# Gathering a token's lower-numbered expert row during the last expert of a two-layer MoE backbone

## The reference, cut to what matters

```
def moe_route(flat, router_w, router_b):
    s = jax.nn.sigmoid((flat @ router_w).astype(jnp.float32))
    ...
    _, idx = lax.top_k(jnp.where(in_group, biased, -jnp.inf), TOP_K)
    w = jnp.take_along_axis(s, idx, axis=-1)
    w = w / jnp.sum(w, axis=-1, keepdims=True)
...
    for e in range(N_EXPERTS):
        hid = jax.nn.silu(flat @ w_gate[e]) * (flat @ w_up[e])
        out = out + combine[:, e:e + 1] * (hid @ w_down[e]).astype(jnp.float32)
...
    x = x + g1 * mx
    x = x + g2 * moe_ffn(...)
```

## Time and profile before

| | us |
|---|---|
| Median of three executions | 1182.84 |
| Lowest and highest | 1179.83, 1184.31 |
| Profiled execution, its own time | 1181.55 |
| Span in its trace | 1179.6 |
| PE busy | 1021.6 (87%) |
| DVE busy | 927.7 (79%) |
| ACT busy | 607.1 (51%) |
| POOL busy | 164.7 (14%) |

### The profile page before, as it was taken

One profiled execution on the slowest core, in us unless ns is written; L12 is line 12 of the kernel. 1 busy time (PEld: TensorE's weight loads), 2 busy tenths in 40 slices (PEclk: granted clock), 3 DMA queues, 4 the chain that ended last, 5 costly groups with the idle time before them and its releaser, 6 DMA issues. The chain is left out here.

```text
span 1179.6 us, 13718 instructions
## 1 busy us (share of the span) xinstructions
PE 1021.6 (87%) x4742; PEld 778.9 (66%) x4742; DVE 927.7 (79%) x1041; ACT 607.1 (51%) x614; POOL 164.7 (14%) x172
## 2 busy tenths in 40 slices
PE   6889999998898982999999999838299999999970
PEld 1466767766565441788888888637278888888860
DVE  4578888877894336699999999655769999999955
ACT  1534222213664113677777777333367777777831
POOL 0100200000100002612212210041341000000005
PEclk9899999998999995899999999959599999999985
DMA  9615878676014004899999999567299999999936
GB/s 372 261 62 208 285 284 302 224 279 232 4 69 134 36 25 155 278 410 414 413 414 414 413 414 414 210 248 278 93 263 404 414 414 414 414 414 414 413 132 234
DMA packets 145692, 332.43 MB, mean 282 GB/s; under 512 B 14064, under 2 KB 16056, under 8 KB 145520
## 3 DMA queue, kind: packets, MB, share of 16 engines
q1 hardware_dynamic: 125768, 277.99, 62.0%
q10 hardware_dynamic: 12392, 28.68, 6.5%
q0 software_dynamic: 7488, 25.19, 5.7%
HBM read 308.72 MB, written 23.15 MB: 281 GB/s over the span
## 5 line engine op out<-in xcount | busy, mean ns | idle before, releaser
L1879 DVE TENSOR_TENSOR w_lo<-ring,w_hi 128x2048 fp32r<-128x2048 f32 x192 | 430.5, 2284 | 24.5 <-ACT w_hi L1725 21.1
L1725 ACT CAST w_hi<-ring 128x2048 fp32r<-128x2048 f32 x192 | 365.3, 1914 | 132.6 <-PE bank L1970 38.7
L1970 PE MATMUL bank<-w_hi,xT_hi 128*128 128x512 f32 x512 | 205.3, 401 | 8.2 <-DVE xT_lo L1886 8.2
L1970 PE MATMUL bank<-w_hi,xT_lo 128*128 128x512 f32 x512 | 201.4, 393 | 0.0
L1970 PE MATMUL bank<-w_lo,xT_hi 128*128 128x512 f32 x512 | 200.9, 392 | 0.0
L1399 PE MATMUL bank<-ring_last_parts,arena_parts 128*128 128x512 f32 (+1 forms) x320 | 116.8, 396 | 5.0 <-DVE ring_parts L1016 2.7
L1970 PEld LDWEIGHTS bank<-w_hi,xT_hi 128*128 128x128 f32 x512 | 97.2, 190 | 30.1 <-DVE xT_lo L1886 9.8
L1970 PEld LDWEIGHTS bank<-w_hi,xT_lo 128*128 128x128 f32 x512 | 96.9, 189 | 21.2
L1970 PEld LDWEIGHTS bank<-w_lo,xT_hi 128*128 128x128 f32 x512 | 97.4, 190 | 19.2
L1074 DVE SCALAR_TENSOR_TENSOR gate_b<-ring,silu_c,gate_b 128x512 f32<-128x512 f32 x140 | 105.9, 756 | 4.5
L1985 PE MATMUL bank<-w_hi,hT_hi 128*128 128x512 f32 x256 | 101.5, 396 | 7.5 <-DVE w_lo L1879 7.5
(11 more groups left out here) (252 smaller groups left out, 1379.3 us busy)
## 6 DMA issues: line engine op xcount, KB each, us to landing
ring<-in_moe_w_gate SPq DMA_DIRECT2D x64, 1024.0 KB, 11.0
ring<-in_moe_w_up SPq DMA_DIRECT2D x64, 1024.0 KB, 13.0
ring<-in_moe_w_down SPq DMA_DIRECT2D x64, 1024.0 KB, 10.7
ring<-in_ada_w SPq DMA_DIRECT2D x21, 2048.0 KB, 8.9
y_scratch<-shared ACTq DMA_DIRECT2D x32, 512.0 KB, 6.0
ring<-in_w_in ACTq DMA_DIRECT2D x21, 512.0 KB, 3.8
shared<-in_ada_w SPq DMA_DIRECT2D x2, 2048.0 KB, 16.0
x_res<-in_x SPq DMA_DIRECT2D x8, 512.0 KB, 12.3
```

The lines of the kernel that those rows point to most:

```text
L1725: nc.scalar.copy(w_hi[:, buf(u, p), :], half(raw(e, p))).then_inc(s_hi, 3 if isinstance(e, int) and (e, p) == (-1, 3) else 1)
L1879: V.tensor_tensor(w_lo[:, buf(u, p), :], half(raw(e, p)), w_hi[:, buf(u, p), :].bitcast(F32), ALU.subtract).then_inc(s_lo, 3 if isinstance ...
L1970: last = pe.matmul(bank[:, b, :], xs[:, kk, :], ws[:, k, :], start=(kk == 0 and i == 0), stop=(kk == KD - 1 and i == 2))
```

## The change

The two experts of a token are put in order of their number: choice 0 is the lower (`e_sel` by min and max instead of by score). The lower one is never expert 15, so its row is in `y_dram` as soon as expert 14 is stored. At the end of `moe(l)` GpSimd waits for that and gathers the four tiles of choice 0 into ring slot 1 (`first_rows`), with an index `row_early` that is held below 15 * 128. In the next block GpSimd gathers only the four tiles of choice 1, while VectorE adds the four tiles of choice 0 (`add_first`), and then those of choice 1 (`add`). In the pooling block the additions now stand ahead of the gating of the pooling weights, and `pool_scale` has a place of its own.

```
+                    pool.wait_ge(s_early, 1)
+                    pool.wait_ge(s_lo, pos_count(NE - 2, 3))
+                    pool.wait_ge(s_yst[0], 16 * (NE // 2 + 1))
+                    pool.wait_ge(s_yst[1], 16 * (NE // 2))
+                    for t in range(NT):
+                        pool.indirect_dma_start(
+                            out=first_rows[:, t, :], out_offset=None, in_=y_dram[0:LAST * P, :],
+                            in_offset=bass.IndirectOffsetOnAxis(ap=row_early[:, t:t + 1], axis=0)).then_inc(early[t], 16)
...
-                        ins = V.tensor_copy(e_sel[:, c, :], top8i[:, :, c])
+                        ins = V.tensor_copy(e_raw[:, c, :], top8i[:, :, c])
+                    link(ins)
+                    for c, pick_of in ((0, ALU.min), (1, ALU.max)):
+                        ins = V.tensor_tensor(e_sel[:, c, :], e_raw[:, 0, :], e_raw[:, 1, :], pick_of)
                     link(ins)
...
                     V.tensor_copy(idx[:], bank[:, 4, NT * NE:NT * NE + 3]).then_inc(s_idx, 1)
+                    V.tensor_scalar(row_early[:], row_tmp[:, 0, 0, :], float(LAST * P - 1), None, ALU.min
+                                    ).then_inc(s_early, 1)
...
                 with pool.Else():
-                    tiles(NE * P)
+                    nc.gpsimd.memset(idx_zero[:], 0.0).then_inc(self.settled, 1)
+                    for t in range(NT):
+                        tile(1, t, NE * P, self.loaded[t])
+
+            def add_one(self, dve, c, t, done):
+
+                nc.vector.scalar_tensor_tensor(x[:, t, :], self.rows[c][:, t, :], weight[:, c, t:t + 1], x[:, t, :],
+                                               ALU.mult, ALU.add).then_inc(done, 1)
+                dve.wait_ge(done, t + 1)
+
+            def add_first(self, dve):
+
+                dve.wait_ge(self.settled, 1)
+                for t in range(NT):
+                    dve.wait_ge(early[t], 16 * (self.l + 1))
+                    self.add_one(dve, 0, t, self.chain)
 
             def add(self, dve, t):
 
-                for c, done in ((0, self.chain), (1, self.done)):
-                    dve.wait_ge(self.loaded[c][t], 16)
...
+                dve.wait_ge(self.loaded[t], 16)
+                self.add_one(dve, 1, t, self.done)
...
+                combine.add_first(dve)
+                for t in range(NT):
+                    combine.add(dve, t)
                 dve.wait_ge(p_ps, 16)
                 link(nc.vector.tensor_tensor(gate1_b[:], gate1_b[:], pool_scale, ALU.mult))
                 for k in range(2):
                     ins = nc.vector.tensor_tensor(pool_w[:, :, k, :], pool_w_raw[:, :, k, :],
                                                   gate1_b[:].rearrange("p (g c) -> p g c", g=len(WINDOWS)), ALU.mult)
                 ins.then_inc(p_wg, 1)
-                for t in range(NT):
-                    combine.add(dve, t)
                 front1.scales(dve)
...
             def _(dve):
+                combine.add_first(dve)
                 combine.add(dve, 0)
                 combine.add(dve, 1)
                 dve.wait_ge(f_ld, 16)
```

More of the change, by code:

```diff
@@ L118, in build_program @@
         half_load = [nc.alloc_semaphore(name=f"half_slot{r}_loaded") for r in range(6)]
+        early = [nc.alloc_semaphore(name=f"first_choice_rows_loaded{t}") for t in range(NT)]
         held = []
@@ L166, in build_program @@
         row_of = sb("row_of", [P, 2, NT], U32)
+        row_early = sb("row_early", [P, NT], U32)
         max_count = sb("max_count", [P, 1], I32)
@@ L1547, in build_program @@
         pool_cols = mod[:].rearrange("p j v -> p (j v)")
+        first_rows = ring[:, 1, :].rearrange("p (t d) -> p t d", t=NT)
         def moe(l):
@@ L2141, in build_program, with __init__ @@
         class Combine:
[L2144 to L2148, removed]
-            def fetch(self, pool):
-                def tiles(written):
-                    for t in range(NT):
[L2154 to L2158, removed]
+            def __init__(self, l, rows):
+                self.l, self.rows = l, (first_rows, rows)
+                c_ = lambda n: sem(f"combine{l}_{n}")
+                self.loaded = [c_(f"rows_loaded{t}") for t in range(NT)]
+                self.again, self.settled = c_("first_rows_loaded_again"), c_("first_rows_settled")
+                self.chain, self.done = c_("first_added"), c_("x_ready")
@@ L2160, in fetch, with tile @@
+            def fetch(self, pool):
+                def tile(c, t, written, loaded):
+                    pool.indirect_dma_start(
+                        out=self.rows[c][:, t, :], out_offset=None, in_=y_dram[0:written, :],
+                        in_offset=bass.IndirectOffsetOnAxis(ap=row_of[:, c, t:t + 1], axis=0)).then_inc(loaded, 16)
                 most = pool.value_load(max_count[0:1, 0:1])
                 with pool.If(most > P):
-                    tiles(LIST_N)
-                with pool.Else():
-                    tiles(NE * P)
@@ L2166, in add @@
-            def add(self, dve, t):
-                for c, done in ((0, self.chain), (1, self.done)):
-                    dve.wait_ge(self.loaded[c][t], 16)
-                    nc.vector.scalar_tensor_tensor(x[:, t, :], self.rows[:, c, t, :], weight[:, c, t:t + 1],
-                                                   x[:, t, :], ALU.mult, ALU.add).then_inc(done, 1)
-                    dve.wait_ge(done, t + 1)
+                    for t in range(NT):
+                        pool.wait_ge(early[t], 16 * (self.l + 1))
+                        tile(0, t, LIST_N, self.again)
@@ new lines, in fetch @@
+                    pool.wait_ge(self.again, 16 * NT)
+                    nc.gpsimd.memset(idx_zero[:], 0.0).then_inc(self.settled, 1)
+                    for t in range(NT):
+                        tile(1, t, LIST_N, self.loaded[t])
+                with pool.Else():
+                    nc.gpsimd.memset(idx_zero[:], 0.0).then_inc(self.settled, 1)
+                    for t in range(NT):
+                        tile(1, t, NE * P, self.loaded[t])
[3 more added lines that the diff above has]
+                dve.wait_ge(done, t + 1)
```

22 lines of the change are left out of this document (12 added, 10 removed).

## The result

| | before | after |
|---|---|---|
| Median (lowest, highest) of 4 executions each, us | 1182.41 (1179.83, 1184.31) | 1192.45 (1191.63, 1197.87) |
| Profiled execution: its own time, us | 1181.55 | 1192.99 |
| Span in its trace, us | 1179.6 | 1191.0 |

The ratio is 1.0093, with an interval of 1.0069 to 1.0118: the change makes the kernel about 0.9% slower. The forecast was 1177.6 in a range of 1173.8 to 1181.5, and slower had 0.06. The forecast is wrong.

The account below looks back on a forecast made before the run. It took the gathers on GpSimd to pace the final block and hold back the additions. Gains of 4.5 (final block) and 1.2 (pooling block) less 0.5 (routing) made 5.2 us, from 1182.84 to 1177.6 us, range 1173.8 to 1181.5.

Parts of the forecast that it names:

- the last sentence on routing: After the routing estimate: added semaphores and memory places were taken to cost nothing that a profile row shows.
- Final block, +4.5: Final block: four fewer gathers on GpSimd and earlier additions gain 4.5 us, bounds 3.7 to 5.0.
- The store and the early gathers, 0 and 0.2: Layer ends: early gathers hidden under the last expert, 0 us; 0.2 us off for expert 15's store meeting the last one.
- Pooling block, +1.2: Pooling block: additions end 5.8 us earlier, but loads behind the gating let only 1.2 us through, bounds 0.3 to 2.4.
- TensorE's pause: Pooling block: TensorE idles 1.8 us ahead of the mixing product instead of 0.44, its clock more likely holding.
- Rival 1: TensorE's clock falls ahead of the mixing product, costing 2.5 us more; gain 2.7, time 1180.1 us; chance 0.17.
- Routing, -0.5: Routing ahead of the first token gather: min, max and one link lose 0.27 us per layer, 0.5 us in all.
- Rival 2: Pooling block: TensorE's columns, not the front's loads, are the limit, gaining 2.6 us there; time 1176.2 us; chance 0.11.
- Rival 3: VectorE's early additions slow GpSimd's late gathers, the fourth issued 3.1 us later; gain about zero, 1182.8 us; chance 0.08.
- Rival 4: Both blocks: late rows land late, no gain at 9.5 us, a 6 us loss at 12.5 (1188.8 us); chance 0.05.

Follow-up runs that it names:

- e2: The kernel before with an unused 32-byte tensor ahead of `ring` and nothing else; 1193.55 us, ratio to before 1.0102.
- e5: The kernel before with the 32-byte tensor `weight` allocated behind `ring`, so `ring` stands 32 bytes lower; 1193.48 us, ratio to before 1.0098.
- e1: The changed kernel with `row_early` in the unused bytes of `max_count`, so `ring` is back in its old place; 1180.11 us, ratio to before 0.9974.
- e12: The kernel of e1 run again, unchanged, beside later runs on one chip; 1179.75 us, ratio to before 0.9968.
- e3: The kernel before with 128 unused bytes ahead of `ring` and nothing else; 1194.82 us, ratio to before 1.0091.
- e6: The kernel before with the 512-byte tensor `ones` allocated behind `ring`, so `ring` stands 512 bytes lower; 1181.08 us, ratio to before 0.9985.
- e8: e1 with the front's scale and shift in memory of their own, loaded after two tiles without waiting for the gating; 1176.55 us, ratio to before 0.9957.
- e11: e1 with early gathers in layer 1 only and the pooling block as before the change; 1178.50 us, ratio to before 0.9954.
- e10: e8 with three tiles gathered early instead of four, in both layers; 1176.85 us, ratio to before 0.9941.
- e7: e1 with the pooling block's gating put between the early and the late additions; 1180.55 us, ratio to before 0.9980.

## Why the prediction was wrong

**The failed step** is the last sentence on routing: "Semaphores and memory places cost nothing that a row shows." It is true to the letter, since no row of before shows an address, and it cost 10.2 us (5.7 and 4.5), twice the gain that the sum gave. e2 and e5 show the cost without anything else of the change, e1 the change without the cost. I had priced each instruction that the change moves and no instruction that it leaves alone. The terms that I did price were off as well, as the next part says, but without this one the kernel would have been faster than before (e1).

**The rest, with `ring` in place,** gained 3.1 us in the first comparison (0.9974 of some 1183, with 0.9 to 5.3 by its interval) and 3.8 in the second (0.9968, 1.9 to 5.7), where 5.2 was forecast. The stretches of the table say where the terms were off:

- **Final block, +4.5.** The block gained 3.4 in after, under the bounds of 3.7 to 5.0, and 4.2 and 4.3 in e1 and e12, inside them. But it starts later.
- **The store and the early gathers, 0 and 0.2.** The early gathers started 3.5 us (layer 1) and 5.5 us (layer 0) behind the issue of expert 14's store (1150.29 and 760.25), not 2.7. The profile puts both down to the split of expert 15's up weights (`<-DVE w_lo`), but the store is what they wait for: in all 15 places of the traces the first early gather starts 0.85 to 0.87 us behind the landing of that store, both where the first of the two splits ended with the landing (layer 1 of after: 1153.06 and 1152.94) and where it ended 1.9 us ahead of it (layer 0: 763.01 and 764.91), and in layer 1 the second split runs on until 1155.26. I had put 0.1 us there. The 5.5 us come from the store itself, which took 4.7 us to land; in layer 0 of e2, e3 and e5, which have no early gathers, it took 4.5 to 4.9, and in all kernels with `ring` at a multiple of 256 it took 2.6 to 2.9. That the slower weight stream is still in its way there is likely and not shown. In layer 1 the first gather lasts 2.27 us, beside the second split. That leaves the last one's landing beside expert 15's store, which then took 3.6 to 4.6 us to land in nine of the eleven such places, where it took 2.6 before. The block behind starts 1.3 and 1.2 us late in after, up to 2.0 in e1. I had bounded it at 0.6 and counted 0.2 in one layer, because I asked only whether the early rows land before the block can end, and not what they do to the store that ends it.
- **Pooling block, +1.2.** Measured -1.4, and by the table's columns -1.0 and -1.2 in e1 and e12. The clock took 1.6 to 1.7, routing 0.3, and the columns of VectorE came 0.24 early, not 1.5; that makes -1.7 in after, 0.3 more than measured, which is within what this stretch varies by in kernels that don't change it (73.1 before, 73.5 in e6, 73.7 to 73.9 in e2, e3 and e5). I had the right wait, the loads behind `p_wg`, but was 1.3 us short on it: the fourth late addition ended 12.98 us behind the block's start, not 12.05, the loads were issued 0.87 later than I put them, and the last took 6.3 us, not 6.0.
- **TensorE's pause.** I put it at 1.8 us and it was 3.65, because the pooling product began 2.9 us early, as forecast, and also ran shorter (9.98 against 10.54), and the loads came late on the other side. Rival 1 came true, at 1.7 us of the 2.5 it was given. The Trainium skill's rule on the gate ("TensorE: Matmul & The Clock Gate", Part 1), that idleness lowers the clock, agrees with the rows: 0.60 behind a pause of 3.65 us, and 10.60 us for the product behind 0.44. Of the pauses ahead of a product, 2.5 us left the clock up, and 3.65, 3.92 and 4.01 did not: the chance of 0.17 was too low mainly because the pause was sized too low.
- **Routing, -0.5.** The two instructions and their link took 0.26 us in layer 0 of after (min and max start at 454.00, the next group at 454.26), as forecast (0.27).
- **Rival 2** was a matter of the waits, not the landing: e8 takes the loads out of the chain and the block is 3.7 us shorter than before, where rival 2 had 2.6 less 0.3 for routing. The columns of TensorE were ready still earlier than it assumed.
- **Rival 3** came true in small: the first late gather took 1.50 us and the others 1.01, beside the additions, and the fourth is issued 0.7 us later than at 1.24 apiece, not 3.1. My argument against it went by the earlier trace rows, whose 0.93 to 0.94 us are those of layer 0. In layer 1 of before two gathers beside additions took longer too, the eighth (1.05 us) and this one:

```profile
1162.00 1.63 POOL L2155 DMA_INDIRECT shared<-y_scratch,row_of  x1 [0.30 <-issue]
```

What decides is when a gather starts. Of the 208 gathers of result rows in the thirteen traces, the 87 that started while VectorE ran nothing took 0.93 or 0.94 us, also where a VectorE instruction began during them. Of the 121 that started in the midst of a VectorE instruction, 116 took 0.94 us plus what that instruction had left to run less 0.13 us, where it had more left than that, each to within 0.01 us: 1.63 for an addition with 0.82 us left, 1.50 with 0.69, 1.01 with 0.20, and 2.27 beside a split with 1.45. Four others started within 0.06 us of the VectorE instruction's own start and took 0.94, and one (e11, 1.97 us) started 0.03 us ahead of the next instruction. So a gather waits for the VectorE instruction that runs when it starts. The Trainium skill ("SBUF — State Buffer", "SBUF: two separate sides") has a VectorE instruction with two SBUF inputs and a GpSimd instruction that reads SBUF lock each other out, and these traces agree: the additions and splits have two such inputs. It costs 0.56 us for the first late gather and 0.07 for each other.
- **Rival 4** did not come: the landings of the late gathers in after were 4.9 to 6.5 us.

With `ring` in place the time is 1180.1 and 1179.8 (e1, e12), inside the range. By these medians the terms of the sum were off by 1.4 to 2.1 us together, and the missing term by 10. The stretches say more. Those outside the loops add up to 105.7 us before and 106.4 in e6, and to 104.7 in e1 and 105.8 in e12: a gain of -0.1 to 1.7 us, where the sum had 5.4 for them (4.5 and 1.2, less 0.3 for the routing of layer 1). One profiled execution of each can't settle which is nearer, and why they differ stays open; so the terms were off by at least 1.4 us and maybe by 5. e10, without the collision and with the loads free, takes 99.0 us in these stretches, 6.7 less than before, and by its median 7.0. The range was drawn from the work on the path and had no term for a change of allocation.

## What to carry to other kernels

When an edit adds a small tensor, write down which large transfer targets move and what their start is modulo 256 bytes, before any row is priced; allocate small tensors behind the big stream buffers or into unused bytes. In a loop where TensorE is full and the stream's landing times leave little slack, a few per cent of stream rate come back as a per cent of the kernel. Freed work ahead of a wait is worth what the next wait lets through: ask of every load that it needs on what its issue waits, and whether a gap that opens ahead of a product is long enough to cost its clock.

## What the runs showed of the hardware

- **A destination off a 256-byte multiple slows a stream of plain transfers from DRAM into SBUF.** 414 GB/s became 399, with `ring` at a remainder of 0 (before, e1, e6 to e12) and of 32, 128 and 224 (after and e2, e3, e5), and the kernel 0.9 to 1.0% slower. These are transfers of 1 MB, in packets of 2048 and 4096 bytes, and a packet takes some 3.5 and 5 ns longer (84.0 to 87.5, 159.0 to 164.0). The Trainium skill ("DMA: Bandwidth & Descriptors", "How a descriptor splits into AXI transactions") says, of what a descriptor fetches, that one that doesn't start at a multiple of 256 bytes begins with a transaction from the multiple below, and pays for the bytes ahead of it in beats of 32 bytes. By its beats a piece of 2048 bytes would cost 1, 4 and 7 beats more than 64, which is 1.6%, 6.3% and 10.9%, an estimate from that page; the rows have 4.0% to 4.5% for all three. They agree that the start matters and differ on how: the remainder hardly does. Which part of the path wants the extra time stays open, and so does whether the source's place matters alike, which wasn't tried.
- **A pause costs its product more than its length.** After 3.65 to 4.01 us the next product of 10.60 us took 12.18 to 12.29 us, and e7 shows that a kernel that starts this product at the same place without the pause gets the 1.6 us back.
- **An indirect gather on GpSimd waits for the VectorE instruction that is running when it starts**: alone it took 0.94 us, behind an addition up to 1.94, and beside a split 2.02 to 2.30, with the exceptions named above.
- **The profiled executions differ ahead of the first layer** by more than the changes here are worth (460.8 to 469.9 us at the first token gather, in nine kernels with `ring` in place; 463.7 and 465.9 in e12 and e1, which are one kernel), while a loop of 303 us repeats to within 0.7 us in nearly all traces (302.5 to 303.2 in 17 of 18 loops with `ring` in place; one had 301.7). The stretches tell apart what medians can't.
